# Even layer of a three-part sequence model on one core: copies issued in another order, low parts on another engine, one gelu in a later step

## The reference, cut to what matters

```
q, k, v, gate_a, u, gate_b = split_cols(hn @ w_in, EVEN_SPLITS)
q = rms_norm(q, q_g); k = rms_norm(k, k_g)
att = swa_sink_attention(q, k, v, sinks, rel_bias) * silu(gate_a)
ssm = s5_mixer(u, ...) * silu(gate_b)
return concatenate([att, ssm]) @ w_out

# s5_mixer: a diagonal complex state-space scan over 32 groups of 16 channels, then
y = gelu(y)
h = y @ glu_w + glu_b
return h[..., :W] * sigmoid(h[..., W:])
```

## Time and profile before

| what | value |
|---|---|
| runs | 2211.40, 2212.49, 2216.36 us; median 2212.49 |
| profiled execution | 2213.06 us, span 2211.8 us |
| mean granted clock of TensorE | 0.965 |
| TensorE busy | 2061.3 us (93%) |
| VectorE busy | 1403.5 us (63%) |
| ScalarE busy | 847.6 us (38%) |
| GpSimd busy | 729.8 us (33%) |

### The profile page before, as it was taken

One profiled execution on the slowest core, in us unless ns is written; L12 is line 12 of the kernel. 1 busy time (PEld: TensorE's weight loads), 2 busy tenths in 40 slices (PEclk: granted clock), 3 DMA queues, 4 the chain that ended last, 5 costly groups with the idle time before them and its releaser, 6 DMA issues.

```text
span 2211.8 us, 24392 instructions
## 1 busy us (share of the span) xinstructions
PE 2061.3 (93%) x9344; PEld 1579.8 (71%) x9344; DVE 1403.5 (63%) x2024; ACT 847.6 (38%) x1417; POOL 729.8 (33%) x529
## 2 busy tenths in 40 slices
PE   7998986999999999899999999999999898998996
PEld 5787764788657666566678787888776676776885
DVE  6365559412154879555416799899995766763547
ACT  5333257423354773145422333444222223451431
POOL 3566612354201111255435100000004764225545
PEclk9999998999999999999999999999999998999999
DMA  4312230244220112211042311111232214345322
GB/s 161 118 54 82 87 127 15 86 143 148 72 76 20 48 48 76 89 54 49 29 151 87 114 40 58 48 57 57 92 108 71 63 43 147 125 166 205 105 77 105
DMA packets 71341, 193.73 MB, mean 88 GB/s; under 512 B 10990, under 2 KB 20367, under 8 KB 70968
## 3 DMA queue, kind: packets, MB, share of 16 engines
q1 hardware_dynamic: 71224, 192.16, 25.7%
HBM read 148.70 MB, written 46.71 MB: 88 GB/s over the span
## 4 chain that ended last, share of the span: by engine, by line
PE 65%; DVE 16%; ACT 5%; POOL 4%; DMA 4%; issue 4%; SPq 1%; DVEq 0%; POOLq 0%; ACTq 0%
PE psum L262 61%; DVE m L2718 3%; PE psum L265 3%; POOL m L307 2%; DMA m<-in_w 2%; DVE m L2739 1%; DVE m L1061 1%; DMA scr_hscr<-m 1%; DVE m L1042 1%; PE psum L1822 1%; DVE m L1949 1%; ACT m L297 1%; DVE m L2796 1%; ACT m L391 1%; DVE m L317 1%
## 5 line engine op out<-in xcount | busy, mean ns | idle before, releaser
L262 PE MATMUL psum<-m,m 128*128 128x512 f32 (+8 forms) x8436 | 1937.3, 396 | 83.4 <-POOL m L307 20.1
L262 PEld LDWEIGHTS psum<-m,m 128*128 128x128 f32 (+3 forms) x8436 | 1469.3, 190 | 527.2 <-issue 154.6
L307 POOL TENSOR_TENSOR m<-m,m 128x1024 fp32r<-128x1024 f32 (+1 forms) x126 | 314.8, 2502 | 1080.2 <-ACT m L297 1080.0
L2718 DVE SCALAR_TENSOR_TENSOR m<-m,m,m 128x1024 f32<-128x1024 f32 x240 | 308.2, 1286 | 6.3
L297 ACT ACTIVATE m<-m 128x1024 fp32r<-128x1024 f32 (+2 forms) x166 | 173.5, 1049 | 343.9 <-PE psum L262 220.7
L265 PE MATMUL psum<-m,m 128*128 128x128 f32 x848 | 128.1, 292 | 53.3 <-DVE m L1042 19.2
L265 PEld LDWEIGHTS psum<-m,m 128*128 128x128 f32 x848 | 106.0, 151 | 77.0 <-ACT m L1312 26.1
L1949 DVE TENSOR_SCALAR_CACHE_REDUCE m<-m,m 128x896 bf16<-128x896 f32 (+4 forms) x130 | 102.7, 846 | 1.0
L2073 DVE CUSTOM_DVE_ANT_0 m<-psum,m 128x128 f32<-128x128 f32 (+3 forms) x64 | 48.2, 755 | 54.1 <-POOL m L2274 21.8
L2274 POOL TENSOR_TENSOR m<-m,m 128x384 f32<-128x384 f32 (+5 forms) x48 | 72.1, 1521 | 10.6 <-DVE m L2073 10.6
L2179 ACT ACTIVATE m<-m,m 128x1024 bf16<-128x1024 f32 (+1 forms) x62 | 64.1, 1037 | 24.3 <-DVE m L1976 24.3
(11 more groups left out here) (300 smaller groups left out, 1698.3 us busy)
## 6 DMA issues: line engine op xcount, KB each, us to landing
m<-in_w SPq DMA_DIRECT2D x164, 512.0 KB, 3.4
scr_hscr<-m SPq DMA_DIRECT2D x4, 2048.0 KB, 6.7
m<-scr_hscr SPq DMA_DIRECT2D x4, 2048.0 KB, 12.1
scr_turned<-scr_strip SPq DMA_DIRECT2D x8, 575.5 KB, 12.8
m<-in_x SPq DMA_DIRECT2D x8, 512.0 KB, 7.5
scr_gscr<-m SPq DMA_DIRECT2D x16, 256.0 KB, 4.2
m<-in_x SPq DMA_DIRECT2D x2, 2048.0 KB, 7.9
m<-scr_turned SPq DMA_DIRECT2D x8, 512.0 KB, 3.5
```

Of the source, the lines that this page charges most:

```text
L262: return self.nc.tensor.matmul(out, lhsT, rhs, start=start, stop=stop, skip_group_check=True)
L307: k.nc.gpsimd.tensor_tensor(lo, raw, hi.bitcast(F32), ALU.subtract).then_inc(*k.up("w_lo", i))
L2718: V.scalar_tensor_tensor(o, u[:, j:j + 1024], w[:, j:j + 1], o, ALU.mult, ALU.add).then_inc(*up("cv_tap", m, j))
```

## The change

1. In the slots, SyncE issues the gate's store and the state-space part (stores, loads, spreads) before the weight panel of the slot, where the panel came first.
2. The three loads of finished state-space outputs stand at the end of slot 22, where they stood in slot 24; the stores of the last two gates of the slots, and of the last set, come after them.
3. The low parts of the four state-space tiles are made on VectorE, in the step in which ScalarE makes the high part; the steps are 6, 7, 8 and 10, where they were 6 to 9. The low part of the attention output's first half is made on VectorE after the loop's step 16, where GpSimd made it in step 15.
4. The fourth gelu stands in step 8, where it stood in step 2.

```diff
+        self.y_steps = [6, 7, 8, 10]
 # VectorE, attention loop
+        if i in E.y_steps:
+            m = E.y_steps.index(i)
+            dve.wait_ge(*at("y_hi", m))
+            yh, yl = (x[:, m, :].rearrange("p (c j) -> p c j", j=8) for x in (E.YH, E.YL))
+            V.tensor_tensor(yl, E.in_turn(m), yh.bitcast(F32), ALU.subtract).then_inc(*up("y_lo", m))
+        if i == n:
+            att_low(0)
 # ScalarE, attention loop
-        if i == 2:
+        if i == 8:
             gelu(3)
-        if 6 <= i <= 9:
-            m = i - 6
+        if i in E.y_steps:
+            m = E.y_steps.index(i)
 # GpSimd, attention loop
-        if 6 <= i <= 9:
-            m = i - 6
-            pool.wait_ge(*at("y_hi", m))
...
-        if i == 15:
-            pool.wait_ge(*at("att_hi", 0))
...
 # SyncE, slots
-        if kind in ("q", "kk", "v") and half:
-            sp_panel(k, 10 + s // 2)
-        elif kind == "g":
-            if half:
-                sp_panel(k, 16 + m)
+        if kind == "g" and s < 23:
             gate_out(m, half)
         n, part = ssm_turn(s)
-        if part == 0 and n:
-            if n == 8:
-                sp.wait_ge(*at("s5_M", 7))
-                sp.wait_ge(*at("s5_PS", 7))
-                sp.wait_ge(*at("s5_K_ps", 7))
-                for m in range(3):
-                    load_y(m)
+        if part == 0 and 0 < n < 8:
             store_y(n - 1)
             if n < 7:
                 load_u(n + 1)
         if part == 1:
             spread_kernel(n)
+        if kind in ("q", "kk", "v") and half:
+            sp_panel(k, 10 + s // 2)
+        elif kind == "g" and half:
+            sp_panel(k, 16 + m)
+        if s == 22:
+            sp.wait_ge(*at("s5_M", 7))
+            sp.wait_ge(*at("s5_PS", 7))
+            sp.wait_ge(*at("s5_K_ps", 7))
+            for tile in range(3):
+                load_y(tile)
+    store_y(7)
+    for _, m, half in E.slots[23:]:
+        gate_out(m, half)
```

More of the change, by code:

```diff
@@ L1475, in pool_even @@
             pool_panel(k, 14 + E.late_gate(i)[1])
-        if 6 <= i <= 9:
-            m = i - 6
-            pool.wait_ge(*at("y_hi", m))
-            yh, yl = (x[:, m, :].rearrange("p (c j) -> p c j", j=8) for x in (E.YH, E.YL))
-            G.tensor_tensor(yl, E.in_turn(m), yh.bitcast(F32), ALU.subtract).then_inc(*up("y_lo", m))
-        if i == 15:
-            pool.wait_ge(*at("att_hi", 0))
-            G.tensor_tensor(E.half(E.ML, 0), E.half(E.GA, 0), E.half(E.MH, 0).bitcast(F32), ALU.subtract).then_inc(*up("att_lo", 0))
     k.mark("ev_att")
```

## The result

The changed kernel takes 2205.25 us (median of 7 runs, 2203.51 to 2209.16) against 2213.21 us for the kernel before (7 runs, 2209.96 to 2216.36). The ratio is 0.9965 with the interval 0.9953 to 0.9977: 7.7 us faster, between 5.1 and 10.4. A second series gave 0.9958 (0.9942 to 0.9974). The measured time lies about midway between the forecast and rival B's 2202.7, so the time alone does not choose between the two; the traces do.

What follows compares the result with a forecast made beforehand. Three timelines decide: SyncE's queue around the spreads, ScalarE's around the gelus, VectorE's in the attention loop. −7.4 − 5.1 − 2.6 − 3.7 − 2.4 + 16.3 = −4.9 us gave 2207.6 us; range 2200 to 2216 us.

Steps and rivals of the forecast that it cites:

- rival B: Strided subtraction in the attention loop takes 1.2 us (−3.2), full clock in 308 to 316 us (−1.7): 2202.7 us; chance 0.22.
- Spreads and the clock behind them: TensorE's two waits for spreading copies go, 7.4 us; the matmuls behind them run at full clock, 5.1 us.
- A: The clock is not given back behind TensorE's removed waits: 7.5 us missing, 2215.1 us; chance 0.20.
- C: Another wait replaces that for the spreads, so neither the 7.4 nor the 5.1 us come: 2220.1 us; chance 0.08.
- Outputs sooner: Earlier state-space output loads offer up to 4.9 us before the late gate's tanh; TensorE's gate product limits the gain to 2.6.
- Gelu out of step 2 and the clock: Attention step 2 loses ScalarE's gelu and table loads, 3.7 us; TensorE's low clock behind the wait goes, 2.4 us.
- Low parts on VectorE: In four attention-loop steps VectorE waits for ScalarE's high part, making steps serial at 10.74 us: +16.3 us.
- waited for by nobody in these rows: State-space stores and loads passing the weight panel in the other slots were costed at nothing.
- the 5.1 us: Behind the two copy waits, 24 matmuls take 2.92 in place of 5.46 us if TensorE is not idle.
- y: Time of VectorE's strided low-part subtraction in the attention loop: taken as 2.0 us, bounds 1.20 and 2.88 us.

Runs made afterwards that it cites:

- Copies only: The kernel before with SyncE's new order alone (spreads ahead of panels, three output loads in slot 22): 0.9937, 14.0 us faster.
- busy wait: The kernel before with four extra 128x512 matmuls ahead of the outputs of state-space sets 4 and 6, results overwritten: 0.9966, 7.5 us faster.
- spreads only: The kernel before with the spreads ahead of the panels alone, the three output loads left where they stood: 0.9938, 13.7 us faster.
- gelu in step 2: The kernel after with the fourth gelu moved back from step 8 to step 2: 0.9999 against the kernel before.

## Why the prediction was right, step by step

- **Spreads and the clock behind them**, −12.5: in the trace −6.6 (205 to 220 us) and −5.7 (220 to 271), −12.3. "Copies only" shows the two together, the busy wait the clock by itself. Nothing took the place of the wait, and the clock is 1.00 behind it: rivals A and C are out.
- **Outputs sooner**, −2.6: −2.6 in after's trace from 300 to 308 us, 2.0 up to 330 us by "spreads only" but 0.6 up to 410 and 0.3 timed. The limit was TensorE's gate product, as said.
- **Gelu out of step 2 and the clock**, −6.1: from 308 to 330 us −6.2 in the trace; together with the price in step 8 the traces give 4.0 us for the move, the timed runs 7.5 (3.7 to 11.3). The 2.3 us in step 8 came as worked out (12.92 against 10.62).
- **Low parts on VectorE**, +16.3: +15.9. The low part took 1.91 us for the 2.0 taken, a step 10.62 for 10.74. Rival B's 1.2 us is the contiguous one, and its full clock behind the halved wait did not come either (0.79 in 296 to 304 us); it came with that wait filled. B's 2202.7 us is as near to the measured time as the forecast, but neither of its causes took place.
- **What the sum lacked**: +1.3 us at 181 us. The other slots' spreads are not in the sum at all; what I wrote off as "waited for by nobody in these rows" were only the stores and loads. In slot 7 the earlier spreads bring TensorE 0.3 us sooner to a wait for VectorE, it is idle for 1.84 in place of 1.53 us, and the 24 matmuls behind take 1.6 us more. I had also read the full clock near there as evidence for the 5.1 us, without seeing how little was in hand at this wait.
- **The range.** The forecast's own range for y from 1.2 to 2.88 us is 2204.4 to 2211.1 us (2207.6 − 3.2 and + 3.5); the prediction wrote 2203.5 to 2211.5. Nothing else rests on it.
- **What stays open.** Over 178 to 410 us the trace gives −5.3 + 1.3 = −4.0 us, close to the forecast −4.9, and the timed runs −7.7 and −9.3. The −9.3 are of after timed once more in a later series. I had expected a ratio of 0.998 there, as if the traces told all; it came to 0.9958, a miss. All thirteen series came out further below before than their traces' windows give, by 0.2 to 5.4 us (mean 1.9).
- **The executions behind the traces.** Before's profiled execution took 2213.06 us, against a median of 2215.04 over the 56 runs of the three later series. After's two took 2208.49 and 2208.00, some 3 us above the medians of their series, 2205.25 and 2204.98. Run by run, the time goes with the mean granted clock: in before, 0.001 less goes with about 1.3 us more. The traces of both kernels have 0.965 or 0.966, but the timed runs have 0.9647 on average for before, 0.9670 for after and 0.9621 for "gelu in step 2". The 0.0023 between before and after are about 3 us (an estimate from these runs), which is most of the gap. Why the clock is higher in after's timed runs than in its traces, and lower with the gelu in step 2, nothing here shows.
- **The way to the end.** That a saving ahead of 410 us reaches the end one to one, as the sum takes it, single traces do not show: behind 410 us, where all kernels are the same, they differ by some 4 us either way.
- **Luck.** The mechanism is right term by term. That the total came within 2.8 us of the timed gain is in part luck, since the sum lacks the 1.3 us, and between 3 and 4 us of the timed gain belong to none of its terms.

By its trace the change as a whole is three good parts, worth about 21 us, and one that gives 16 of them back: the experiments keep the former at 2192 us by moving the low parts one step.

## What to carry to other kernels

When work moves to an engine with an in-order list, ask whose result it waits for: a low part in the step of its high part closes a loop over two engines and costs 10.6 us a step here, the same instruction one step later 6.6. A wait of TensorE costs more than itself when the clock falls behind it; the trace shows it as two times for the same matmuls (5.46 and 2.92 us here), and filling the wait with needless matmuls tests it. And look at the next wait behind a saving: TensorE reached the one at 181 us 0.3 us sooner, waited 0.3 us longer, and the matmuls behind it took 1.6 us more.

## What the runs showed of the hardware

Extra matmuls in front of two waits for copies made the kernel before 7.5 us faster (4.4 us in the trace), with a granted clock of 1.00 in place of 0.53 behind the first. Over the 56 runs of before, a mean granted clock lower by 0.001 goes with about 1.3 us more. An idle time of 1.53 us left the granted clock at 1.00, one of 1.84 us at the same place was followed by 0.72 in 184 to 190 us (0.72 to 0.87 in the ten traces with such an idle time). VectorE's subtraction of 128x1024 took 1.91 us where one operand was read in steps of 512 bytes and 1.23 us where it was contiguous; GpSimd's 2.85 to 2.88 us with the stride. With the low parts on GpSimd the first step of VectorE beside such a subtraction took 7.35 in place of 4.74 us, and three scalings in it 3.48 in place of 0.88 us. On ScalarE, the row behind each ACT_TABLE_LOAD of 1.28 us in "gelu in step 2" started 0.01 us after its end.
